# Modulation products on TensorE, the attention input product by pairs of blocks, and normalizations that hand over pairs of blocks, in a two-network forward pass on one Trainium2 core

## What is computed

```python
def first_block(...):
    for i in range(DEPTH):
        shift, scale, gate = ada_modulation(c, ada_w[i, 0], ada_b[i, 0])   # silu(c) @ w + b
        h = x * (1.0 + scale) + shift
        y = windowed_gqa(h, ...) if i == 0 else recurrent_block(h, ...)
        x = layer_norm(DN_ALPHA * x + (1.0 + gate) * y, ln_g[i, 0], ln_b[i, 0])
        shift, scale, gate = ada_modulation(c, ada_w[i, 1], ada_b[i, 1])
        y = sq_relu_mlp(x * (1.0 + scale) + shift, mlp_w1[i], mlp_w2[i])
        x = layer_norm(DN_ALPHA * x + (1.0 + gate) * y, ln_g[i, 1], ln_b[i, 1])
    return x
# second network: x = x + grid_sincos(L); hx = rmsnorm(x) * (1 + scale) + shift; zx = hx @ w_in ...
```

## Time and profile before

| | us |
|---|---|
| median of 3 runs (lowest, highest) | 1612.23 (1610.78, 1612.74) |
| the profiled execution's own time | 1610.23 |
| its span, first to last instruction | 1608.9 |
| TensorE busy with matmuls | 1359.3 (84%) |
| VectorE busy | 1124.6 (70%) |
| ScalarE busy | 698.6 (43%) |
| GpSimd busy | 62.3 (4%) |
| mean granted TensorE clock | 0.936 |

### The profile page before, as it was taken

How to read it: one execution, slowest core, us unless ns; L and a number is a source line. 1 busy time by engine, 2 the same in 40 slices (tenths; PEclk the granted TensorE clock), 3 DMA queues, 4 the chain that set the end, 5 groups by cost and what they waited for, 6 DMA issues and landing times.

```text
span 1608.9 us, 20642 instructions
## 1 busy us (share of the span) xinstructions
PE 1359.3 (84%) x7720; PEld 1175.1 (73%) x7720; DVE 1124.6 (70%) x1509; ACT 698.6 (43%) x887; POOL 62.3 (4%) x54
## 2 busy tenths in 40 slices
PE   0867699997999977998974998765769999999996
PEld 0756599996777756998973787654667777777874
DVE  6656677776677666777786647885566767767675
ACT  2331344441665762444442433210225656656553
POOL 2100100001000001000000000231000000000000
PEclk9989899999999978999997998987769999999998
DMA  9426677773566646655660345200024887879662
GB/s 365 144 98 242 204 262 262 290 289 115 196 245 213 209 157 239 250 209 221 222 215 8 130 158 197 66 1 3 9 104 145 282 305 246 292 252 330 232 239 110
DMA packets 84068, 311.89 MB, mean 194 GB/s; under 512 B 9344, under 2 KB 9568, under 8 KB 83360
## 3 DMA queue, kind: packets, MB, share of 16 engines
q1 hardware_dynamic: 82080, 298.88, 52.3%
q10 hardware_dynamic: 1888, 11.69, 2.2%
HBM read 309.48 MB, written 1.05 MB: 193 GB/s over the span
## 4 chain that ended last, share of the span: by engine, by line
PE 65%; DVE 23%; ACT 5%; DMA 4%; issue 2%; POOL 0%; SPq 0%; DVEq 0%; ACTq 0%; POOLq 0%
PE ps L406 64%; DVE w_low L365 5%; DVE junk L365 4%; DMA ring<-moe 2%; ACT w_high L365 2%; DMA ring<-stream 2%; DVE t_one L365 1%; DVE t_two L365 1%; DVE rs L365 1%; DVE x L365 1%; DVE qp L365 1%; DVE pf L365 1%; DVE r_two L365 1%; DVE sc L365 1%; ACT h_high L365 1%
## 5 line engine op out<-in xcount | busy, mean ns | idle before, releaser
L365 DVE TENSOR_TENSOR w_low<-ring,w_high 128x1024 fp32r<-128x1024 f32 x356 | 437.0, 1228 | 174.3 <-ACT w_high L365 150.1
L365 ACT ACTIVATE w_high<-ring 128x1024 fp32r<-128x1024 f32 x356 | 377.6, 1061 | 317.5 <-PE ps L406 175.5
L406 PE MATMUL ps<-x_high,w_high 128*128 128x256 f32 (+1 forms) x784 | 236.3, 301 | 80.3 <-DVE x_low L365 71.5
L406 PE MATMUL ps<-x_low,w_high 128*128 128x256 f32 (+1 forms) x784 | 233.4, 298 | 0.0
L406 PE MATMUL ps<-x_high,w_low 128*128 128x256 f32 (+1 forms) x784 | 233.3, 298 | 0.0
L406 PEld LDWEIGHTS ps<-x_high,w_high 128*128 128x128 f32 x784 | 154.9, 198 | 92.0 <-issue 85.7
L365 DVE CUSTOM_DVE_ANT_0 junk<-ring,cond 128x1024 f32<-128x1024 f32 x125 | 155.5, 1244 | 23.4 <-DMA ring<-stream 8.3
L406 PEld LDWEIGHTS ps<-x_low,w_high 128*128 128x128 f32 x784 | 155.0, 198 | 2.6
L406 PEld LDWEIGHTS ps<-x_high,w_low 128*128 128x128 f32 x784 | 154.6, 197 | 2.8
L406 PE MATMUL ps<-h_high,w_high 128*128 128x256 f32 x512 | 145.9, 285 | 3.6 <-DVE w_low L365 2.0
L406 PE MATMUL ps<-h_low,w_high 128*128 128x256 f32 x512 | 145.0, 283 | 0.0
(11 more groups left out here) (299 smaller groups left out, 2094.3 us busy)
## 6 DMA issues: line engine op xcount, KB each, us to landing
ring<-stream SPq DMA_DIRECT2D x376, 512.0 KB, 4.7
ring<-moe SPq DMA_DIRECT2D x192, 512.0 KB, 4.6
tab_two<-tab ACTq DMA_DIRECT2D x1, 2824.0 KB, 15.4
gw<-gw ACTq DMA_DIRECT2D x1, 2304.0 KB, 14.0
cond<-cvec ACTq DMA_DIRECT2D x3, 512.0 KB, 6.8
x<-xT ACTq DMA_DIRECT2D x1, 1024.0 KB, 11.9
ctx<-ctxT ACTq DMA_DIRECT2D x1, 1024.0 KB, 4.8
pos<-posT ACTq DMA_DIRECT2D x1, 1024.0 KB, 7.6
```

Of the source, the lines that this page charges most:

```text
L365: return op(*a, **k).then_inc(self.sem, 1)
L406: return pe.matmul(out, stationary, moving, start=start, stop=stop, skip_group_check=True)
```

## The change

1. **Modulation on TensorE.** The first 32 `a` pieces (kind `e`) are laid out transposed on the host and multiplied on TensorE: `ada_piece` makes eight float32 matmuls, each with a 128 x 128 block of the piece as the stationary side and one column of silu(c) (`cond_cols`) as the moving side. 16 of them stand ahead of and between the products of attention's input, 16 in the attention. VectorE's and GpSimd's work on these pieces goes.
2. **Input product by pairs.** Attention's input weight comes as 12 pieces, one for each pair of blocks `k` and third of the columns (A: tiles 0 to 3, B: 4 to 7, C: keys and values). All ten tiles and the values accumulate at once in six PSUM banks; pair `p` can start when its own four `e` pieces are done. The rotations come at the end, in the order of `ROPE`.
3. **Normalizations by pairs.** `normalized` multiplies a block with its factor and with `rs` in one VectorE instruction, ScalarE adds the shift while it makes `x_high` (`shifted`), and `x_low` follows pair by pair. Scaling of the mean is folded into the subtraction. The positional table is added in the last layer norm.
4. **First tiles by pairs.** `first_tiles` runs three tiles of an MLP's first product together over each pair; the recurrent block's first and the second network's first two tiles likewise.
5. **Early sums.** The last piece of a second product signals after blocks 2, 4 and 6 (`sums`), so that `evacuate` can start.
6. **Moves.** `next_x` goes from GpSimd to VectorE (`T1` times factor and `rs`) and ScalarE (shift); the recurrent block's constants from the start to the output product of attention; two splits of the MLP's first weights ahead of the last residual addition.

```diff
-    order = pieces("a" * 8 + "w" * 6 + "a" * 8 + "wa" * 4 + mlp)
+    order = "e" * 8 + "www" + "eeee" + "www" + "eeee" + "w" * 6 + "e" * 16 + pieces("wa" * 4 + mlp)
...
+    def ada_piece(n, out):
+        c = ADA_AT[n]
+        pe.wait_ge(arrived[c % RING], 16 * (c // RING + 1))
+        for k in range(KT):
+            ins = mm(out, m.piece(c)[:, k * P:(k + 1) * P], m.C8[:, k:k + 1], k == 0, k == KT - 1)
+        ins.then_inc(s.ada_pe, 1)
...
+    def heads(p, part, tiles):
+        w = QKV_AT[p, part]
+        pe.wait_ge(s.w_low, split_upto(w + 1))
+        pe.wait_ge(s.x_low, p + 1)
+        for tile in tiles:
+            for k in range(2):
+                lo = k * 512 + (tile - 4 * "ABC".index(part)) * P
+                ins = mm3(PS[:, tile // 2, (tile % 2) * 256:(tile % 2 + 1) * 256], weight(w, lo), pair(XIN, slice(None), 2 * p + k),
...
+    first_modulation(0)
+    first_modulation(1)
+    for part in QKV_PARTS[0]:
+        columns(0, part)
+    first_modulation(2)
+    columns(1, "A")
+    first_modulation(3, (0, 1))
+    columns(1, "B")
+    first_modulation(3, (2, 3))
+    columns(1, "C")
+    for part in QKV_PARTS[2]:
+        columns(2, part)
...
+    def first_tiles(w0, x_low):
+        for p in range(4):
+            pe.wait_ge(s.x_low, x_low + p)
+            for n in range(3):
...
@@ scalar_program
+    high_x(0)
+    high_x(1)
+    act.dma_start(m.TAB, tab).then_inc(s.in_att, 16)
+    act.dma_start(m.ident, ident_d).then_inc(s.in_att, 16)
+    high_upto(W_QKV + 3)
+    high_x(2)
+    high_upto(W_QKV + 6)
+    high_x(3)
+    high_upto(W_ATT)
@@ vector_program
+    def normalized(n, src, scale, shift):
+        def scaled(p):
+            for k in (2 * p, 2 * p + 1):
+                op(vv.scalar_tensor_tensor, m.T2[:, k, :], src[:, k, :], scale[:, k:k + 1], m.RSTD, ALU.mult, ALU.mult, inc=s.t2 if k % 2 else None)
...
+    first_modulation(0)
+    first_modulation(1)
+    low_upto(W_QKV + 3)
+    first_modulation(2)
+    low_upto(W_QKV + 6)
+    first_modulation(3)
+    low_upto(W_ATT)
```

More of the change, by code:

```diff
@@ L108, in stream_order @@
     assert len(order) == 2 * N_CHUNKS
-    out, n = [], {"w": 0, "a": 0, "p": 0}
-    for piece in range(2 * N_CHUNKS):
-        kind = "p" if piece in POOL_PIECES else order[piece]
+    out, n = [], {"w": 0, "a": 0, "e": 0}
+    for kind in order:
         out.append((kind, n[kind]))
@@ L225, in __init__ @@
         self.junk_rnn = view("junk_rnn", aXL, 1024)
-        self.ada_halves = [view("ada_half", aT1 + 1024 * j, 1024) for j in range(2)]
+        self.C8 = view("cond_cols", aX + 4096 - 8, 8)
         a0 = aB + 1056
@@ L417, in pair, with out_tile @@
         return hl[0][ix], hl[1][ix]
-    def out_tile(w, out, src, x_low=None, order=range(KT)):
+    def out_tile(w, out, src, order=range(KT), fresh=True):
         pe.wait_ge(s.w_low, split_upto(w + 1))
         for k in order:
-            if x_low is not None and k % 2 == 0:
-                pe.wait_ge(s.x_low, x_low + k // 2)
-            ins = mm3(out, weight(w, k * P), pair(src, slice(None), k), k == order[0], k == order[-1])
+            ins = mm3(out, weight(w, k * P), pair(src, slice(None), k), k == order[0] and fresh, k == order[-1])
         ins.then_inc(s.used, 1)
@@ new lines, in values, with columns @@
+    def values(p):
+        w = QKV_AT[p, "C"]
+        for b in range(2):
+            for k in range(2):
+                ins = mm3(PS[:, 5, b * 256:(b + 1) * 256], pair(XIN, slice(None), 2 * p + k, slice(b * P, (b + 1) * P)), weight(w, k * 512 + 256, 256),
+                          p == 0 and b == 0 and k == 0, p == 3 and k == 1)
+        return ins
+    def columns(p, part):
+        if part == "C":
+            heads(p, part, (8, 9))
+            values(p).then_inc(s.used, 1)
+        else:
+            first = 4 * "ABC".index(part)
+            heads(p, part, range(first, first + 4)).then_inc(s.used, 1)
@@ new lines, in rotate, with modulate @@
+    def rotate(r):
+        n2 = ROPE[r]
+        if r == 0:
+            pe.wait_ge(s.in_att, 32)
+        pe.wait_ge(s.qk_out, r + 1)
+        if r >= 2:
+            pe.wait_ge(s.rope_ps, r - 1)
+        mm(PS[0:32, 6 + r % 2, :], m.tab("roper", 32), m.QK[0:32, 2 * n2:2 * n2 + 2, :], True, True).then_inc(s.rope_mm, 1)
+    batches = ((0, 0), (0, 1), (1, 0), (1, 1))
+    PV_BANK = (0, 1, 3, 0)
+    beside = iter(range(2 * E_CHUNKS - 16))
+    def modulate(n):
+        for _ in range(n):
+            j = next(beside)
+            ada_piece(16 + j, PS[:, 2, j:j + 1])
@@ L548, in mlp @@
             t = t0 + i
+            if i == 0 and x_low is not None:
+                if t >= 1:
+                    pe.wait_ge(s.relu, 2 * t)
+                first_tiles(w0, x_low)
             for a in range(2):
@@ L639, in tensor_program @@
     filters_after = {1: (0,), 2: (1,), 3: (2,), 4: (3,), 5: (4, 5), 6: (6, 7)}
-    for t in range(8):
+    for p in range(4):
+        pe.wait_ge(s.x_low, x_splits(MOD_POS) + p + 1)
+        for t in range(2):
+            if p == 0:
+                pe.wait_ge(s.w_low, split_upto(W_IN2 + t + 1))
+            for k in (2 * p, 2 * p + 1):
+                ins = mm3(PS[:, t, :].rearrange("p (s t) -> p s t", s=2), weight(W_IN2 + t, k * P), (m.XH[:, :, k, :], m.XL[:, :, k, :]), k == 0, k == KT - 1)
+            if p == 3:
+                ins.then_inc(s.used, 1)
+    filters(0)
+    for t in range(2, 8):
         bank = t % 4
```

408 lines of the change are left out of this document (240 added, 168 removed).

## The result

The changed kernel takes 1632.99 us (median of 4 runs, 1630.84 to 1636.27), the kernel before in the same comparison 1611.51: ratio 1.0144, 95% interval 1.0128 to 1.0160. It is slower by 1.4%. Its profiled execution has a span of 1630.0 us, 21.1 more than before.

The account below looks back on a forecast made before the run. VectorE's chain set the attention's pace; the bound moves to TensorE. +16.1 to the scores, +21.8 attention, -5.1, -2.7, -2.2 and -6.9 at the norms make +21.0: 1631.2 us, median 1633, own range 1621 to 1648, overall 1600 to 1648.

Parts of the forecast that it names:

- The price of a piece: Modulation on TensorE: 16 records a piece, 3.42 us at 1.2 GHz, 1.72 at 2.4; later pieces 2.57 on average.
- narrow products do as little for the clock as idling: Modulation on TensorE: runs of narrow products lose the upper clock level, so half the later pieces are priced at either level.
- Rival A: Start and attention: the upper clock level, once lifted, is kept through narrow runs; faster, median 1606 us; chance 0.27.
- rival B: Start and attention: narrow products cost 1.7 us a piece from the first; faster, median 1588 us; chance 0.08.
- The point at which a later piece turns the sign: Start and attention: the change turns from slower to faster at about 2.0 us for a later modulation piece.
- The chain behind the pieces: Start: small VectorE operations, modulations, splits, semaphores and DMA issues between the first eight pieces and the first product, 4.8 us.
- The waits for the copies: Input product: five waits in the old order, 1 us or more each, saved inside the new order.
- the 1.4 us of waits that I kept: Attention: TensorE waits for the first softmax and last copy that were to stay, 1.4 us.
- The other norms: Layer norms after the first: second -2.7 us, third -2.2, last norm and the one behind it -6.9.
- 0.3 lost: First MLP: three tiles together free weight slots late, so ReLU and the next split come behind the fourth tile; 0.3 us.
- 3.0 through: Second MLP: next_x puts 4 us of work on VectorE where TensorE waits for w_low; 3 us lengthen the time.
- rival D: Norms: they do not give what they promise, half of the 17 us lost; slower, median 1642 us; chance 0.08.

Follow-up runs that it names:

- e1: The changed kernel with the moving column of every modulation product repeated to 128 columns: 1596.47 us, ratio 0.9928 to the kernel before.
- e2: The changed kernel with the moving column of every modulation product repeated to 64 columns: 1607.59 us, ratio 0.9992 to the kernel before.
- e5: e1 with ScalarE and VectorE splitting the input product's next weight pieces ahead of the pair that would wait for them: 1581.36 us, ratio 0.9832 to the kernel before.
- e7: The kernel before with only normalizations and first tiles by pairs, shift on ScalarE, early sums and next_x moved: 1597.99 us, ratio 0.9935, span 1593.2 us.
- e9: e5 with next_x taken off VectorE and ScalarE and given to GpSimd: 1582.93 us, ratio 0.9827 to the kernel before.

## Why the prediction was right, and where it was off

**The price of a piece.** Held in both numbers: 3.43 us for each of the first eight (27.47 / 8; forecast 3.42), and for the eight later ones of the start 10.73 + 3.79 + 4.83 = 19.4, 2.42 each for 2.57. That narrow products do as little for the clock as idling was a choice between two ends; the window 48.5 to 57.6 shows the fall, and e1 shows that it decides the sign. Rival A (1606) and rival B (1588) are the times forecast for a kernel without this loss: e2, with the clock held but not lifted, came out at 1607.59, and e1, with both, at 1596.47, 8 us above B. The point at which a later piece turns the sign is 1.9 us by the prediction's own sums, and not 2.0.
The Trainium skill, page "TensorE: Matmul & The Clock Gate", section "LDWEIGHTS (loading the stationary operand)", gives the load a price that does not depend on the clock; the records of the first 27 us, at 0.215 us each against 0.107 at the upper level, do not bear it out for float32.

**Start and input product.** First product 36.88 for 37.4, scores 106.63 for 106.1. The chain behind the pieces was 4.62 us for 4.8. It was taken as given; e5 shows that it could be avoided. The waits for the copies in the old order, "1 us or more each" in the prediction, were 0.7 to 0.8 us; the sum does not use them.

**Attention.** 68.5 us for 71.2. The 16 pieces took 39.6 us for 41.1, and the 1.4 us of waits that I kept did not come: the timeline from 106.63 to 175.10 has no gap.

**Normalizations.** First -5.5 for -5.4; the reciprocals to the products 5.0 as worked out. The other norms, with the recurrent block, gave 2.3 us more than forecast, 1.9 of it in the recurrent block and the norm behind it.

**The MLPs: the mis-sized term.** The step "0.3 lost" for late slots, and "3.0 through" for `next_x` in the second MLP alone, were too small. From first to last product the first MLP took 4.1 us more (220.53 to 411.35, before 190.35 to 377.1) for +0.3, the second 7.6 us more (218.7 for 211.1) for +3.3. I had priced VectorE's new work by what TensorE already waited for there, and the trace of before had no such wait in the first MLP; and I had put the late slots at 0.3 where the first split behind the product starts 3.6 us later than before (10.2 for 6.6). The waits for `w_low` and `h_low` are 3.2 us of the 4.1 and 5.3 of the 7.6; the rest was not traced. Of that rival D had the place but not the size: the second half alone is worth 15.7 us by its span (e7).

**Unforeseen gain.** From the second network's first product to the end 3.4 us were won, which I had at 0. The part up to the router took 297.1 to 300.3 us in the kernels with the new normalizations and 300.8 before, in bursts of small products whose clock differs from trace to trace. What moves it wasn't tried.

The sum came out right (+21.1 for +21.0) since some 8 us too little in the MLPs stood against 2.7 too much in the attention, 2.3 more gained in the norms and 3.4 unforeseen at the end. The mechanism was right; that the total is so close is luck.

## What to carry to other kernels

Before you move a matrix-vector product onto TensorE, look what it does to the clock of the work around it: here it was cheap in time and dear in clock, and repeating the vector's column up to the width of the load cost almost nothing (it turned +1.4% into -0.7%). Then look at every wait on TensorE of some us: it can be paid twice, by itself and by the lower level behind it, so that moving the splits ahead of data they don't need gave 14 us for 9.8 us of waits. And tiles that run together over each pair give back the slots of their weights together, and late; look what waits for these slots behind them.

## What the runs showed of the hardware

- Without a gap between them, products of one column ran while the granted clock fell from 1.00 to 0.50 (46.9 to 52 us), though the profile shows TensorE as fully busy. With 128 columns it rose from idling within the first run of pieces (128 records in 16.36 us for 27.47).
- With 64 columns the upper level stayed behind wide products (64 records in 7.26 us) and did not come from idling: 27.57 us for the first eight pieces, as one column (27.47).
- A float32 record with 128 columns of load took 0.107 us at 2.4 GHz and 0.215 at 1.2 with one moving column, and 0.110 to 0.112 at 2.4 GHz with 128.
- GpSimd's passes over 128 x 256 in e9 took 0.56 to 0.78 us at first and 1.05 to 1.79 from 181 us on, beside VectorE's first turn; VectorE's four `x_low` beside the first of them took 3.27 us for 2.12 in e5, and `h_low` came later: TensorE's first two waits were 0.72 and 1.05 us for 0.33 and 0.58 in e5.
